# Memory keys and values projected inside the scan's sample step, and an opening by token blocks

## The reference, cut to what matters

```python
x = x + 0.5 * swiglu(rmsnorm(x, g_ffn1), w1_gate, w1_up, w1_down)       # width 2816
mix, ... = token_mix(rmsnorm(x, g_mix), ...)     # pooling mixer and state-space scan, then w_out
x = x + mix
x = x + cross_attn(rmsnorm(x, g_xq), k_mem, v_mem, w_xq, w_xo)
x = x + 0.5 * swiglu(rmsnorm(x, g_ffn2), w2_gate, w2_up, w2_down)

def mem_kv(mem, g_mem, w_mem_k, w_mem_v):        # for the prompt group: 256 memory rows
    m = rmsnorm(mem, g_mem)
    return (m @ w_mem_k).reshape(...), (m @ w_mem_v).reshape(...)       # both are outputs too
```

## Time and profile before

| | us |
|---|---|
| median of 3 runs (lowest, highest) | 2562.58 (2560.77, 2566.39) |
| profiled execution, its own time | 2562.23 |
| its span, first to last instruction | 2560.5 |
| PE busy | 2406.7 (94%) |
| DVE busy | 1315.8 (51%) |
| ACT busy | 544.2 (21%) |
| POOL busy | 130.5 (5%) |

### The profile page before, as it was taken

The page is one execution under the profiler, slowest core; times in us unless marked ns, Lnnn a source line. Parts: engine busy times, 40 slices in busy tenths (PEclk is TensorE's granted clock), DMA queues, the critical chain, the costliest instruction groups (busy, mean ns, idle before and its releaser), DMA issues.

```text
span 2560.5 us, 36291 instructions
## 1 busy us (share of the span) xinstructions
PE 2406.7 (94%) x14674; PEld 2303.1 (90%) x14674; DVE 1315.8 (51%) x2357; ACT 544.2 (21%) x852; POOL 130.5 (5%) x127
## 2 busy tenths in 40 slices
PE   5799999999999989889879998899999999999998
PEld 4689999999999979776558997699999999999998
DVE  3664444444444786523786834427544444444445
ACT  3511111111111411021221304214111111111112
POOL 4300000000000000002430000000000000000000
PEclk9899999999999989985979999999999999999999
DMA  5411111111111311112012333321111111111111
GB/s 183 133 50 34 49 49 49 40 42 49 49 49 50 99 42 51 34 53 64 17 40 66 103 116 132 116 91 44 50 47 36 49 49 49 35 47 49 49 33 68
DMA packets 175256, 157.27 MB, mean 61 GB/s; under 512 B 6163, under 2 KB 158305, under 8 KB 174777
## 3 DMA queue, kind: packets, MB, share of 16 engines
q1 hardware_dynamic: 175169, 156.05, 19.6%
HBM read 136.18 MB, written 19.94 MB: 61 GB/s over the span
## 4 chain that ended last, share of the span: by engine, by line
PE 84%; DVE 12%; issue 2%; ACT 1%; DMA 1%; POOL 0%; SPq 0%; DVEq 0%; ACTq 0%
PE bank L1897 25%; PE bank L1898 24%; PE bank L1899 24%; PE bank L2397 1%; PE bank L2345 1%; DVE h_lo L1118 1%; PE bank L2309 1%; PE bank L2222 1%; PE bank L2357 1%; DVE w_lo L1092 1%; DVE ew L1554 1%; DVE ntmp L1068 1%; DVE ntmp L1069 1%; DVE rb L1070 1%; PE bank L2300 1%
## 5 line engine op out<-in xcount | busy, mean ns | idle before, releaser
L1897 PE MATMUL bank<-h_hi,w_hi 128*128 128x352 f32 x3120 | 1016.6, 326 | 33.9 <-ACT vtok L783 11.5
L1898 PE MATMUL bank<-h_lo,w_hi 128*128 128x352 f32 x3120 | 1005.0, 322 | 0.0
L1899 PE MATMUL bank<-h_hi,w_lo 128*128 128x352 f32 x3120 | 1004.6, 322 | 0.0
L1897 PEld LDWEIGHTS bank<-h_hi,w_hi 128*128 128x128 f32 x3120 | 589.9, 189 | 37.3 <-ACT vtok L783 11.9
L1898 PEld LDWEIGHTS bank<-h_lo,w_hi 128*128 128x128 f32 x3120 | 590.7, 189 | 1.3 <-issue 0.3
L1899 PEld LDWEIGHTS bank<-h_hi,w_lo 128*128 128x128 f32 x3120 | 589.4, 189 | 0.0
L1200 DVE SCALAR_TENSOR_TENSOR x<-bank,x 128x352 f32<-128x352 f32 x528 | 276.0, 524 | 192.7 <-PE bank L1899 192.6
L1897 PE MATMUL bank<-mid_hi,w_hi 128*128 128x352 f32 x1056 | 342.9, 325 | 7.5 <-DVE x L1200 7.5
L1898 PE MATMUL bank<-mid_lo,w_hi 128*128 128x352 f32 x1056 | 340.0, 322 | 0.0
L1899 PE MATMUL bank<-mid_hi,w_lo 128*128 128x352 f32 x1056 | 339.6, 322 | 0.0
L740 ACT ACTIVATE w_hi<-w_raw 128x1024 fp32r<-128x1024 f32 x190 | 192.6, 1048 | 281.0 <-PE bank L1899 182.1
(11 more groups left out here) (302 smaller groups left out, 1698.4 us busy)
## 6 DMA issues: line engine op xcount, KB each, us to landing
w_raw<-in_w_gate_dram SPq DMA_DIRECT2D x44, 512.0 KB, 3.9
w_raw<-in_w_up_dram SPq DMA_DIRECT2D x44, 512.0 KB, 4.6
w_raw<-in_w_down_dram SPq DMA_DIRECT2D x44, 512.0 KB, 3.8
w_raw<-in_w_in_dram SPq DMA_DIRECT2D x18, 512.0 KB, 4.2
x_spill<-x SPq DMA_DIRECT2D x6, 1408.0 KB, 6.2
kring<-in_cache_mem_k_dram SPq DMA_DIRECT2D x8, 1024.0 KB, 4.9
vring<-in_cache_mem_v_dram SPq DMA_DIRECT2D x8, 1024.0 KB, 5.0
x<-x_spill SPq DMA_DIRECT2D x4, 1056.0 KB, 5.1
```

Of the source, the lines that this page charges most:

```text
L1897: eng.matmul(out, a_hi, b_hi, start=first, stop=False)
L1898: eng.matmul(out, a_hi, b_lo, start=False, stop=False)
L1899: return eng.matmul(out, a_lo, b_hi, start=False, stop=last)
```

## The change

1. The sixteen memory units leave the opening. They become two units for the memory rows themselves (U_MEM) and sixteen of another cut (U_KV: two blocks of 128 rows by 512 columns), after w_in. Two raw buffers throughout; POOL splits none; slots 2 to 5 for U_KV.
2. The opening works by token blocks: SP loads three blocks of x, two weight units, the parameters, and the rest between. The row sums of squares come from ACT's accumulator on the untransposed blocks (`x_square`), DVE makes the factor for three blocks at a time on 128 x 3 numbers and three diagonal matrices (`x_stats`), and PE spreads them over the partitions by a product with ones (`x_spread`) into bank 6, copied to rb by DVE (`x_factors`). Chunk 0 (`ffn_start`) begins when three blocks are turned and has the others between its halves.
3. Memory rows: squared by ACT and turned by PE in pair 7, split straight from PSUM with the gain (`mem_split`, `mem_low`); the norm's factor is put on at the eviction of keys and values.
4. `kv_unit` (PE) stands between the sample step's pieces: 0 to 3 after pair 8, 4 to 8 around the first pieces, 9 to 15 in front of the states. Results of each group of four units are evicted by ACT from banks 6 and 7 to kst and stored; keys are turned (`key_turn`, `kt_copy`) and stored.
5. The states are loaded one by one between the units' loads. The first four w_out units are split at the end of the sample step. Some banks change.

The diff, cut to its core:

```diff
-U_K, U_V, U_F1, U_IN, U_OUT, ... = 0, 8, 16, 82, 100, 108, 116, 124
+U_F1, U_IN, U_MEM, U_KV, U_OUT, ... = 0, 66, 84, 86, 102, 110, 118, 126
...
 def wait_slot(eng, w, i):
+    if U_KV <= w < U_OUT:
+        j = w - U_KV
+        if j < 4: eng.wait_ge(p_ready, (48, 54)[j // 2])
+        else: eng.wait_ge(kv_used, j - 3)
+    if U_OUT <= w < U_OUT + 6:
+        eng.wait_ge(kv_used, 16 if k < 2 else 11 + k)
...
 SP, opening
+for t in range(3): xload(t)
+ffn_unit(U_F1, "w1", 0, 0); ffn_unit(U_F1, "w1", 0, 1)
 ten parameter loads
+xload(3); xload(4); ffn_unit 2; ffn_unit 3
+xload(5), (6), (7)           # each waits x_sq and tr_ready of block t - 5
+ffn_unit 4; ffn_unit 5; xload(8)
...
 SP, after w_in
-for k in range(4): unit(U_OUT + k, ...)
+for t in range(2): unit(U_MEM + t, mp[:, t:t + 1, :])
 tail_out(10); tail_out(11)
-eng.wait_ge(z_ready, 6 * NT); h0 load, 3 MB; unit(U_OUT + 4), unit(U_OUT + 5)
+for j in range(4): kv_unit(j)
+eng.wait_ge(p_ready, 54)
+for j in range(4, 8): kv_unit(j); h0_load(2 * j - 8); h0_load(2 * j - 7)
+kv_unit(8); kv_unit(9); kv_out(0); kt_out(0)
+for j in range(10, 14): kv_unit(j)
+kv_out(1); kt_out(1); kv_unit(14); kv_unit(15); kv_out(2)
+unit(U_OUT + 0), unit(U_OUT + 1); kv_out(3); unit(U_OUT + 2 to 5)
...
 ACT, opening
+x_evac(0..2); wait s_parc, tr_act 3
+hi_unit 0; norm_hi(0, k) k < 4; hi_unit 1; wait tr_dve 3; norm_hi(0, k) k >= 4
+x_evac(3); x_square(0); hi_unit 2; x_square(1); hi_unit 3; x_square(2); x_evac(4); x_evac(5)
+wait tr_act 6, tr_dve 6; norm_hi(1, all k); x_square(3..5)
+ffn_turn 0; hi_unit 4; hi_unit 5; x_evac(6); ffn_turn 1; x_square(6)
+x_evac(7); x_square(7); x_evac(8); x_square(8); norm_hi(2, all k); ffn_turn 2 to 5
...
 ACT, w_in: hi_pair(U_IN + 4 + 2 * pair) for pair < 7 only, hi_pair(U_KV) in pair 8
+pair 7: squares of the memory rows after pool_out; mem_split(n - 1) for n = 1, 2
 ACT, scan
+hi_unit(U_KV + 2); the two exp of softplus; hi_unit 3, 4, 5; kv_evict(0)
 five exp; s_dece
+hi_unit 6
 step 0: xb
+hi_unit 7, 8
 exp to ew
+hi_unit 9, 10; kv_evict(1); hi_unit 11, 12
 for b in range(NB): h0T
+    b in (0, 1): hi_unit 13 + b;   b == 2: kv_evict(2), hi_unit 15
+kv_evict(3); hi_pair(U_OUT); hi_pair(U_OUT + 2)
...
 DVE, opening
+x_evac(0..2); par; w_split 0; norm_lo(0, k) k < 4; w_split 1; norm_lo(0, k) k >= 4
+x_evac(3); x_evac(4); w_split 2; w_split 3; x_stats(0); x_evac(5); x_low(1); x_factors(0)
+gate 0, 1; up 0; w_split 4, 5; mid 0; x_evac(6); up 1; x_stats(1); x_evac(7); x_evac(8)
+x_factors(1); gate 2; mid 1; up 2; x_stats(2); x_low(2); gate 3; mid 2; up 3; x_factors(2)
...
 DVE, w_in and scan
+pair 7: mem_low(n - 1) after the evictions of n = 1, 2;  pair 8: w_pair(U_KV), Newton on 128 x 2
+w_split(U_KV + 2), (3) inside softplus; w_pair(U_KV + 4) after it
 make_ud(0)
+w_split(U_KV + 6); kt_copy(0)
 step 0: sm, ew
+w_pair(U_KV + 7)
 ytok, yc_done
+w_pair(U_KV + 9)
 xs
+kt_copy(1); w_pair(U_KV + 11)
 for b in range(NB): h0T
+    b < 3: w_split(U_KV + 13 + b)
+w_pair(U_OUT)
 bx; the additions to h0
+    after j == 2: w_pair(U_OUT + 2)
...
 PE, opening (ffn_start)
+x_turn(0..2); par; x_turn(3)
+gate 0 (each k waits n_lo); x_turn(4); up 0; x_turn(5); gate 1; x_spread(0); x_turn(6)
+up 1; x_turn(7); gate 2; x_turn(8); up 2; x_spread(1); turn 3; x_spread(2); down 0
+turn 4, 5; down 1; down 2
+x_turn: half = 2t, 2t + 1 in bank (4, 5, 7)[half % 3], waits the eviction of half - 3
...
 PE, w_in and scan
+mem_turn(n) after part n = 0, 1 of pair 7      # mem_turn(1) waits w_ready of mem_low(0)
+for j in range(4): kv_unit(j)                  # after pair 8
 step sizes; turn_x(0)
+kv_unit(4); key_turn(0)
 segments(0); scores_bc(0)
+kv_unit(5); kv_unit(6)
 step 0: y products
+kv_unit(7)
 y transposes
+kv_unit(8); key_turn(1)
 turn_state(0)
 for b in range(NB):
+    if b < 7: kv_unit(9 + b)
     turn_state(b + 1); state products of b
...
+def kv_unit(j):
+    hv, s = j // 4, slot_of(U_KV + j)
+    eng.wait_ge(w_ready, U_KV + j + 1)
+    if j % 4 == 0: wait(eng, kv_ev, 2 * hv)
+    for kk in range(2):
+        k, wc = j % 4 * 2 + kk, slice(512 * kk, 512 * kk + 512)
+        for t in range(2):
+            mm = three(bank[6 + t][:, :], mem_hi[:, k, ms], mem_lo[:, k, ms], w_hi[:, s, wc], w_lo[:, s, wc], ...)
+    mm.then_inc(kv_used, 1)
```

More of the change, by code:

```diff
@@ L374, in down_bank, with y_bank @@
             return bank[(4, 5, 7)[dl % 3]]
+        def y_bank(q, g):
+            return bank[(5, 6)[g] if q else (5, 3)[g]]
         def y_group(t):
@@ L901, in _ @@
                                            ACT.Copy, scale=par[:, PSC + i:PSC + i + 1]).then_inc(po_hi, 1)
+                    eng.wait_ge(p_ready, 42)
+                    for t in range(2):
+                        eng.wait_ge(w_dma[ring(U_MEM + t)], ring_count(U_MEM + t))
+                        eng.activation(msq[:, t, :], raws[ring(U_MEM + t)][:, :], ACT.Square, accum_out=nrm[:, 3, t:t + 1])\
+                           .then_inc(m_sq, 1)
                 for n in range(NT):
+                    if pair == 7 and n:
+                        if n == 1:
+                            eng.wait_ge(m_sq, 2)
+                        mem_split(n - 1)
                     if pair >= 6:
@@ L913, in _, with kv_evict @@
                             eng.activation(d, d, ACT.Silu).then_inc(xbc_ready, 1)
+            def kv_evict(hv):
+                eng.wait_ge(kv_used, 4 * hv + 4)
+                eng.wait_ge(m_rs, 1)
+                if hv in (1, 2):
+                    eng.wait_ge(kt_ready, 2 * hv)
+                wait(eng, s_kvout, 16 * hv)
+                for t in range(2):
+                    eng.activation(kst[:, t, :], bank[6 + t][:, :], ACT.Copy, scale=nrm[:, 1, t:t + 1]).then_inc(kv_ev, 1)
+            hi_unit(U_KV, 2, 0)
             eng.wait_ge(s_dexp, 1)
@@ L943, in _ @@
                 else:
+                    hi_unit(U_KV, 7, 0)
+                    hi_unit(U_KV, 8, 0)
                     eng.wait_ge(seg_ready, 1)
-                    eng.activation(ew[0:NS, 0:HEADS * NS], bank[2][0:NS, 0:HEADS * NS], ACT.Exp).then_inc(e_done, 1)
+                    eng.activation(ew[0:NS, 0:HEADS * NS], bank[3][0:NS, 0:HEADS * NS], ACT.Exp).then_inc(e_done, 1)
+                    hi_unit(U_KV, 9, 0)
+                    hi_unit(U_KV, 10, 0)
+                    kv_evict(1)
+                    hi_unit(U_KV, 11, 0)
+                    hi_unit(U_KV, 12, 0)
                     for b in range(NB):
@@ L1170, in ffn_gate, with x_factors, x_low @@
+            def x_factors(g):
+                a, b = 3 * P * g, min(3 * P * (g + 1), T)
+                eng.wait_ge(x_bc, g + 1)
+                link(eng.tensor_copy(rb[:, a:b], bank[6][:, 0:b - a]))
+                eng.sem_inc(x_rb, 1)
+            def x_low(n):
+                eng.wait_ge(tr_dve, 3 * n + 3)
+                for k in range(KT):
+                    norm_lo(0, n, k, x, G1)
             def ffn_gate(f, i, t):
@@ L1910, in _, with x_spread @@
+            def x_spread(g):
+                eng.wait_ge(x_dg, 3 * g + 3)
+                wait(eng, x_rb, g)
+                for c_ in range(3):
+                    M = P if 3 * g + c_ < 8 else NS
+                    mm = eng.matmul(bank[6][:, c_ * P:c_ * P + M], ones[0:M, :], diag[0:M, c_ * P:c_ * P + M], start=True,
+                                    stop=True)
+                mm.then_inc(x_bc, 1)
             eng.wait_ge(s_const, 5)
+            for t in range(3):
+                x_turn(t)
@@ L2138, in _ @@
                         tail_turn(11)
+                    if n < 2 and pair == 7:
+                        mem_turn(n)
                 if pair == 0:
```

647 lines of the change are left out of this document (386 added, 261 removed).

## The result

Four runs of the changed kernel gave a median of 2527.36 us (2523.90 to 2528.93), four of the kernel before 2562.93 us (2560.77 to 2566.39): a ratio of 0.9858, 95% interval 0.9841 to 0.9875, 1.4% faster. The profiled execution took 2528.93 us, with a span of 2527.2. The forecast was 2518 (2500 to 2541), faster with 0.94. The profiled span fell by 33.3 us; the sum had said 43.8.

The account below looks back on a forecast made before the run. PE was taken as the bound (busy 690 of 695 us in ten middle feed-forward chunks), so only other stages counted. Terms -84 - 3 + 5.2 + 29 + 8 + 1 = -43.8 took 2562.2 to 2518 us, range 2500 to 2541.

Parts of the forecast that it names:

- The opening: Kernel start through chunk 0: first feed-forward product from 104.0 to 13.8 us (-90.2), chunk 0 +6; together -84 us.
- the load sentence: Opening loads: first two weight units land at 9.6 us and the parameters behind them at about 10.
- The stop before block 7's second half: Chunk 0: PE stalls 6 us for ACT's late eviction that frees the bank for token block 7's second half.
- The pool outputs: Around the pool outputs: two w_out splits move behind the eviction PE waited 5.55 us for; -3 us.
- Pairs 7 and 8: Projection, pair 7: 16 added memory transposes, 2.1 us, and a wait for mem_low(0), about 3.1 us; +5.2 us.
- The step up to the last state product: Sample step with sixteen key/value units: 79.4 us against 50.5, with 10 us of PE waits in six places; +29 us.
- supply bound: Rival, sample step: each of the 12 units after the first four costs 5.5 us; 2540 us, chance 0.2.
- From there to the first update: Last state product to first h0 update: 13 us against 5, for evictions, splits and w_pair(U_OUT) ahead of bx; +8 us.
- Updates cold: Twelve h0 updates of the sample step: again at 1.2 GHz, as in their earlier 20.84 us; 0 us.
- clock regained: Rival, sample step: units keep 2.4 GHz, short wait before updates, updates at 0.87 us each; 2503 us, chance 0.2.
- Slower than before: Rival, sample step: the clock falls and the units never bring it back; 2580 us, +0.7%, chance 0.05.
- Behind the step, 0: Scan behind the sample step's h0 updates: taken as unchanged, with no term in the sum; 0 us.

Follow-up runs that it names:

- evict_ahead: Changed kernel with ACT evicting block 6 right behind the products of columns 1 and block 7 right behind the two weight splits: 2522.30 us.
- again: The changed kernel measured once more with no edit: 2525.89 us, ratio 0.9853 to the kernel before.
- turn_behind: Changed kernel with pair 7's transposes of the second memory block put behind the products of columns 2 instead of columns 1: 2519.40 us.
- fill_rest: Changed kernel with 44 unused products of 512 columns on PE while it rests before the h0 updates: 2524.93 us.
- w_out_later: Changed kernel with par_ahead, evict_ahead (also DVE's block 6), turn_behind, bx_early, keys' second half evicted earlier, and w_pair(U_OUT) between the h0 adds: 2505.91 us.
- half_products: Changed kernel with the sixteen key/value units issuing 6 of their 12 products, loads, splits, evictions and transposes kept: 2522.36 us.
- bx_early: Changed kernel with DVE's two bx products moved from behind w_pair(U_OUT) to ahead of kt_copy(1): 2518.67 us.
- par_ahead: Changed kernel with SP asking for the ten small parameter loads ahead of the two weight units: 2525.23 us.
- dense_between: w_out_later with two unused products of 512 columns behind each of the twelve h0 updates: 2521.01 us.

## Why the prediction held, and where it was off

The forecast's mechanism and its sign were right, and the result lies in the range; its value was 9 us too low.

- **The opening** was right to 2.7 us (-81.5 against -84.2). Its start came 3 us late. The term that failed is the load sentence, "the parameters behind them at about 10": bytes alone were counted, and SP's issue itself stood 3.58 us behind 2.5 MB already asked for, so they landed at 13.1. (Its rate of 1.4 us for 512 KB divides 4 MB by the whole time from the issue; between the two landings it read, the row gives (15.71 - 9.31) / 6 = 1.07. Nothing turned on it, as the weights didn't come last.) The stop before block 7's second half is there, 5.05 us against 6; evict_ahead shows that it was ACT's order, and that DVE was only 1.6 us less late. The 4 us of waits for h_lo in the first half didn't come: PE doesn't wait between 16.76 and 37.8. In their place the first twelve products run 0.30 us apart at 0.50 and not 0.16, 1.7 us more, and 1.2 go to a wait for DVE; that chunk 0 came out at +5.7 against +6 is in part luck.
- **The pool outputs**: -3 was a size too large. PE waits 3.65 us for the eviction in place of 5.55 and restarts 1.9 us sooner, but 1.1 of these are lost by the next z: in the two stretches of 4 us that begin 1 us behind the restart the grant is 0.50 and 0.87 (again), where before it was 0.63 and 1.00.
- **Pairs 7 and 8**: the 3.1 us wait for mem_low is 3.0. What it left out is that the clock falls in it, 1.5 us more; turn_behind takes back both.
- **The step up to the last state product**: 81.7 us against 79.4 (from the end of the projection, 1066.2, as the forecast counted from 1141.6); PE waits for 9.6 of it, in four places and not six, and the wait for kv_evict(1) is 6.0 against 4.7. The rival "supply bound" is not borne out in size, since the units behind it run at 4.77 us a pair with their state.
- **From there to the first update**: 10.9 against 13 (the same end, "+8"), since ACT's last eviction and its first two splits (1145.66 to 1148.8) lay partly beside the last state's products; DVE's split pair took 5.20 and bx 5.74, as priced. The two errors cancel: +37.3 against +37.
- **Updates cold**: right, and settled by fill_rest and w_out_later against the rule that was weighed with them. The rival "clock regained" had its first part right (the units keep 1.00) and its last wrong: with bx out of POOL's way and the splits behind the adds (w_out_later) PE rests no more than 0.2 us, and the updates are cold still.
- **Slower than before**: it needed the units at 0.50. half_products shows how near that was: with the units' products halved, 22 us of units and states run at 0.50. In the changed kernel it did fall twice in the step's middle (0.84 over 1080.7 to 1112) and came back each time, which the rival said it would not.
- **Behind the step, 0**: this is the second step that failed, by 5.0 us, 4.6 of them by the scan's end. The scan's steps were taken as unchanged because no instruction of theirs is; their grant is not the same. It costs 116.3 us from the last update to the scan's end in before, 120.7 in again, 118.0 in turn_behind and 118.1 in bx_early, the last three of them kernels that differ only ahead of it (before has as many instructions there, and its grant is 0.88 against 0.85). What in their timing decides which stop drops the grant stays open: no edit was found that moved it at will.

## What to carry to other kernels

Dense work moved between light pieces can lift the clock of both, so that it costs less than its own time, and leaving some of it out can give back what it saves (22 us of products less: the step 2.3 us longer, the whole at most a few us shorter). When work is moved, cost SP's own issue time behind the bytes already asked for, and look at each engine that must evict for one buffer, since removing the latest only shows the next. The grant around short stops in a later, untouched stage can change its price by some us (3.6 between again and evict_ahead, 5.2 between two kernels that are the same up to there); read a gain up to the end of the stage that was edited, and no further.

## What the runs showed of the hardware that was not expected

- The grant falls with PE fully busy in light matmuls: 16.70 of 16.70 us at 0.50 in fill_rest, right behind 10 us at 1.00.
- Two products of 512 columns behind each such update don't keep it: 36.3 us for twelve, at 0.50 from the second on (dense_between).
- SP's issue of a 4 KB load takes 0.38 us behind 1.5 MB of loads asked for just before (par_ahead), 3.58 behind 2.5 MB (3.45 in again).
- Two kernels that are the same up to there took 890.90 and 896.07 us for the same 5,420 matmuls, with the grant at 0.99 and 0.98 (w_out_later and dense_between, one profiled execution each).
- Beside POOL's products a DVE instruction with two operands in SBUF takes 2.6 (w_lo, alone 1.2) to 2.9 us (bx, alone 1.18), one with an operand in PSUM its usual 0.69 (w_out_later, 1136.15). The Trainium skill (SBUF — State Buffer, "Who interferes with whom") has the first contend and the second not; both rows agree with it.
